# Gate-row riders moved to one per chunk, their total into the value stage, and a shorter rotation

## Chip, cores, metric

The kernel runs on one core of one Trainium2 chip. The metric is device time in microseconds (us) for one execution; lower is better.

## The reference

Two transformer-like blocks run on x of 256 tokens by 2048 features, in float32. The first block has two layers. Each modulates its normalised input and weighs its output with a gate that comes from a condition vector c:

```python
def first_block(x, c, ...):
    cond = jax.nn.silu(c)
    for i in range(DEPTH):                      # 2 layers: pool, then sparse attention
        mod = cond @ mod_w[i] + mod_b[i]
        shift, scale, gate = jnp.split(mod, 3, axis=-1)
        h = rms_norm(x, norm_g[i]) * (1.0 + scale[:, None, :]) + shift[:, None, :]
        ...
        x = x + gate[:, None, :] * out
    return rms_norm(x, final_g)

def rope_partial(x, positions, rot_dim):
    ...
    x1, x2, rest = xf[..., :half], xf[..., half:rot_dim], xf[..., rot_dim:]
    out = jnp.concatenate([x1 * cos - x2 * sin, x2 * cos + x1 * sin, rest], axis=-1)
```

The attention layer projects h to q, k, v, a gate (through silu) and indexer queries, keys and weights, rotates q, k and the indexer's parts, picks 64 keys per query and attends. The second block is an mLSTM branch and an attention branch side by side (q and k there are rotated over the whole head dimension of 128), and a feed-forward part with 8192 hidden features.

`mod_w[1]` has 2048 rows by 3 x 2048 columns. Its last third, times cond, is the gate row of the attention layer: the row that this change is about. It is needed first after attention, in the output projection.

## The kernel before

**Chunks and blocks.** All large products are float32 products made of three reduced-precision ones (high x high, low x high, high x low: L1890, L1891, L1892). A weight matrix comes in blocks of 2048 rows by 512 columns, a block in 8 chunks of 256 rows (512 KB). For each chunk SyncE issues the load into one of 8 slots of `raw` (L350), ScalarE writes the high part `w_hi` (L514), VectorE the low part `w_lo` (L1040), both with four slots, and TensorE multiplies. Queues are in order. ScalarE and VectorE work three chunks ahead of the block that TensorE is in (AHEAD = 3): a block's helper `blk` handles chunks 3 to 7 of its block and 0 to 2 of the next. In the code `o` counts 3 to 10; `hooks[o]` is other work put behind the parts of chunk o.

**Stages around the change.** idx_q (2 blocks), idx_kw (a narrow block of 80 columns), qk (8 blocks), gate (4), v (4), attention with 16 heads, attn_out. After each qk block ScalarE brings the result to `stage`, VectorE rotates it (`rotate`), and in the next block TensorE transposes it after chunk 3 and VectorE copies it out after its own chunk 5 (L1122).

**Riders.** The products of cond with `mod_w` that make shift and gate rows mostly don't run on TensorE. VectorE does them piece by piece between its low parts: a rider (L1282) takes a piece of 128 x 1024 (512 KB) from `ride_raw`, scales it by a value per partition and adds it to an accumulator, for this row `wide`. The row of unit 5 (the attention layer's gate row) has 32 riders, in the gate stage (RIDERS = {"gate": 5}). At the end `total_rows` adds up the 128 partitions with four products against ones (L2014, eight recorded matmuls), ScalarE copies the result to `wide` (L781) and stores it in four pieces to `gate_row`, from where it is later spread to all partitions.

**SyncE's queue in the gate stage.** `ride_raw` has four slots. The queue is in this order: the 8 weight loads of gate block 0, then rider loads 0 to 7, then for blocks 1 to 3 in turn weight load, rider load, weight load, rider load, and then the value stage's loads:

```python
            def ride(u, b, j):

                sp.wait_ge(mod_used, b * CPB + (RIDE[u] + j - 3))
                sp.dma_start(ride_raw[:, j % 4:j % 4 + 1, :], piece(u, b, j)).then_inc(ride_landed[j % 4], 16)
...
                    with sp.Fori(1, n) as b:
                        for j in range(CPB):
                            load(src, b, j, b + B0, cols=cols)
                            if u:
                                ride(u, b, j)
```

`mod_used` counts the riders done, so rider load c (c = 8b + j) waits until riders 0 to c-4 are done. A weight load waits for the low part that last used its slot, eight chunks back.

**VectorE in the gate stage.** `phase("gate")` first runs riders 0, 1 and 2 in a row, then the low part of chunk 3 and rider 3, the low part of chunk 4 and rider 4, and so on. In the last gate block riders stop at chunk 7, so that rider 31 is done ahead of the value stage's first chunks.

Of the kernel before, what the change touches and what calls it, by code (L numbers as in the profile page):

```python
# [9 lines left out]
ALU = mybir.AluOpType  # L10
# [4 lines left out]
NT = S // P  # L15
D = 2048
KC = D // P
NBLK = 512
KPC = 2
CPB = KC // KPC  # L20
RAW = 8
SPL = 4
AHEAD = 3
# [11 lines left out]
DSA_HEADS, MOBA_HEADS, M_HEADS, IDX_HEADS = 16, 8, 4, 16  # L35
# [79 lines left out]
JOBS, SPLITS = {}, {}  # L115
# [62 lines left out]
def build(nc, x, c, positions, norm_g, mod_w, mod_b, pool_w_in, pool_w_grp, pool_scale, pool_w_out, attn_w_in,  # L178
# [3 lines left out]
    with ExitStack() as ctx:  # L182
# [15 lines left out]
        tmp = sb("tmp", [P, 4, S])  # L198
        wide = sb("wide", [P, D])
# [24 lines left out]
        ps = ctx.enter_context(nc.psum_tensor("ps", [P, 8, 512], F32))  # L224
# [50 lines left out]
        tp_ready, tp_evac, xh_ready, x_ready = sem("tp_ready"), sem("tp_evac"), sem("xh_ready"), sem("x_ready")  # L275
# [8 lines left out]
        mod_taken, rows_ready, sum_rows = sem("mod_taken"), sem("rows_ready"), sem("sum_rows")  # L284
# [220 lines left out]
        def _(act):  # L505
            step = Chain(act, act_step)
# [48 lines left out]
            def blk(B, hooks=None, last=False, cols=NBLK, at=AHEAD):  # L555

                if hooks and AHEAD - 1 in hooks:
                    hooks[AHEAD - 1]()
                for o in range(at, CPB if last else CPB + AHEAD):
                    hi(B, o, cols if o < CPB else NBLK)  # L560
                    if hooks and o in hooks:
                        hooks[o]()
# [214 lines left out]
                to_qk(b, b + B0, b + A0)  # L777
            phase("gate", lambda b, B, A: evac(T2[:, :, bass.ds(b * NBLK, NBLK)], A, B * CPB + CPB, ACT.Silu))
            load_table(4, ACT.Exp)
            act.wait_ge(sum_rows, 2)  # L780
            nc.scalar.copy(wide[:, 0:NBLK], ps[:, 4, :]).then_inc(row_ready, 1)  # L781
            act.wait_ge(row_ready, 1)
            for q in range(4):
                act.dma_start(gate_row[:, q * NBLK:(q + 1) * NBLK], wide[32 * q:32 * q + 1, 0:NBLK]).then_inc(row_stored, 16)

            def copy_probs(h, i):

# [15 lines left out]
            def exp_hooks(h0):  # L803
                return {9: lambda: exps(h0, 0), 10: lambda: exps(h0 + 1, 1)}
# [16 lines left out]

            B0, A0, n = PHASES["v"]
            for b in range(n):
                blk(B0 + b, exp_hooks(0) if b == n - 1 else None)
                plain_evac(T3)(b, B0 + b, A0 + b)
            attention(0, DSA_HEADS, "attn", True, PHASES["attn_out"][0])

# [204 lines left out]
        def _(dve):  # L1032
# [44 lines left out]
                dve.wait_ge(x_ready, s + 1)  # L1077
                dve.sem_inc(tp_evac, 1)

            def blk(B, hooks=None, last=False, cols=NBLK, ride=None, b=None, ride_to=CPB + AHEAD, at=AHEAD):  # L1080


                if hooks and AHEAD - 1 in hooks:
                    hooks[AHEAD - 1]()
                for o in range(at, CPB if last else CPB + AHEAD):
                    lo(B, o, cols if o < CPB else NBLK)
                    if ride and o < ride_to:
                        rider(ride, b, o)
                    if hooks and o in hooks:
                        hooks[o]()  # L1090

            def phase(name, each=None, out=None, low=None, per=0, first=None, ahead=AHEAD):


                B0, A0, n = PHASES[name]
                u = RIDERS.get(name)
                if u:
                    for o in range(AHEAD):
                        rider(u, 0, o)
                blk(B0, first, ride=u, b=0, at=ahead)  # L1100
                if each:
                    each(0, A0)
                if n > 1:
                    def hooks(b):
                        return {5: lambda: out(b - 1), 6: lambda: low(b - 1)} if out else None

                    with step.loop(1, n - 1 if u else n, per) as b:
                        blk(b + B0, hooks(b), ride=u, b=b)
                        if each:
                            each(b, b + A0)  # L1110
                    if u:
                        blk(n - 1 + B0, hooks(n - 1), ride=u, b=n - 1, ride_to=CPB)
                        if each:
                            each(n - 1, n - 1 + A0)

            def leave(n, dst, scale=None, shift=None, bank=None):

# [85 lines left out]
            def rotate(src, heads, half, at):  # L1203

                v = src.rearrange("p t (h d) -> p t h d", h=heads)
                n = NT * heads * half
                ta, tb = (tmp[:].rearrange("p f t -> p (f t)")[:, k * 512:k * 512 + n]
                          .rearrange("p (t h d) -> p t h d", t=NT, h=heads) for k in range(2))
                x1, x2 = v[:, :, :, 0:half], v[:, :, :, half:2 * half]
                cosb, sinb = (rot[:, k, :, at:at + half].unsqueeze(2).to_broadcast([P, NT, heads, half])  # L1210
                              for k in range(2))
                step(tt(ta, x1, cosb, ALU.mult))
                step(tt(tb, x2, sinb, ALU.mult))
                step(tt(ta, ta, tb, ALU.subtract))
                step(tt(tb, x1, sinb, ALU.mult))
                step(tt(x2, x2, cosb, ALU.mult))
                step(tt(x2, x2, tb, ALU.add))
                step(nc.vector.tensor_copy(x1, ta))  # L1218


            cos, sin = rot[:, 0], rot[:, 1]
# [51 lines left out]
            def rider(u, b, o):  # L1273

                if o == 0 and isinstance(b, int):
                    dve.wait_ge(bias_landed, 16 * CLEARED[u])
                c0 = b * CPB + o
                at = o % 2 * 1024
                lap = b * 2 + (RIDE[u] // 4 + o // 4 + 1)
                dve.wait_ge(ride_landed[o % 4], lap * 16)  # L1280
                acc = mod_acc[u][:, at:at + 1024]
                stt(acc, ride_raw[:, o % 4, :], csil[:, bass.ds(b * 4 + o // 2, 1)], acc, ALU.mult, ALU.add  # L1282
                    ).then_inc(mod_used, 1)
                dve.wait_ge(mod_used, c0 + (RIDE[u] + 1))
# [181 lines left out]
            blk(B0, {3: start_scores, 6: ki_out, 9: lambda: index_scores(0)})  # L1466
            query_key(0, A0)
            dve.wait_ge(res_stored, 16)
            with step.loop(1, n, 11) as b:
                blk(b + B0, {3: lambda: qi_out_now(b), 5: lambda: qk_out(b - 1), 9: lambda: index_scores(b)})  # L1470
                query_key(b, b + A0)

# [246 lines left out]
            def aqk_out(b):  # L1719
                leave(b + JOBS["a_qk"], feat(2)[:, bass.ds(b * 4, 4), :])  # L1720

            phase("a_qk", rotary_full, aqk_out, lambda b: None, per=7,
                  first={2: lambda: mlstm_stage(0), 5: lambda: mlstm_stage(1), 9: lambda: mlstm_low(0, 6),
                         10: lambda: mlstm_low(1, 4)}, ahead=AHEAD + 2)
            B0, _, _ = PHASES["a_v"]
# [151 lines left out]
        def _(pe):  # L1877
# [43 lines left out]
            def blk(B, A, X, free, hooks=None, ready=None, half=None, at=0):  # L1921


                if hooks and -1 in hooks:
                    hooks[-1]()
                if free:
                    pe.wait_ge(acc_free, A - 1)
                for j in range(at, CPB):
                    if half and j == 0:
                        pe.wait_ge(x_first, half)  # L1930
                    elif ready is not None and j % 2 == (1 if half and j < 2 else 0):
                        pe.wait_ge(x_ready, ready + j // 2 + 1)
                    chunk(B, j, X, KPC * j, A, j == 0, j == CPB - 1)
                    if hooks and j in hooks:
                        hooks[j]()

            def phase(name, X, job=None, first=None, ready=None, half=None, at=0):

                B0, A0, n = PHASES[name]
                blk(B0, A0, X, A0 >= 2, first, ready, half, at)  # L1940
                if n > 1:
                    if A0 < 2:
                        blk(1 + B0, 1 + A0, X, False, {3: lambda: job(0)} if job else None)
                    with pe.Fori(2 if A0 < 2 else 1, n) as b:
                        blk(b + B0, b + A0, X, True, {3: lambda: job(b - 1)} if job else None)
# [64 lines left out]
            def total_rows(u, bank):  # L2010

                pe.wait_ge(mod_used, RIDE[u] + 2 * KC)
                for q in range(4):
                    ins = mm(ps[32 * q:32 * q + 32, bank, :], ones[:, 0:32], mod_acc[u][:, q * NBLK:(q + 1) * NBLK],  # L2014
                             start=True, stop=True)
                ins.then_inc(sum_rows, 1)
# [138 lines left out]
            with pe.Fori(1, n) as b:  # L2155
                blk(b + B0, b + A0, XB, True, {3: lambda: qk_job(b - 1), 5: lambda: index_scores(b)})
            phase("gate", XB, first={3: lambda: qk_job(7)})
            pe.wait_ge(tp_evac, JOBS["qk"] + 8)
            pe.wait_ge(relu_ready, IDX_HEADS)
            total_rows(5, 4)  # L2160

            def logits(h0, i, q, k, rows_of=1):
                h = h0 + i
# [53 lines left out]
            def dsa_logits(i):  # L2217
                if i == 0:
                    pe.wait_ge(row_ready, 1)
                logits(0, i, lambda i, r: qk_t[:, i, :], lambda i, r: qk_t[:, DSA_HEADS + i, :])  # L2220

            B0, A0, n = PHASES["v"]
            for b in range(n):
                blk(B0 + b, A0 + b, XB, True, {4: lambda: dsa_logits(0), 5: lambda: dsa_logits(1)} if b == n - 1 else None)
            attention(0, DSA_HEADS, "attn", dsa_logits, lambda i, u: T3[:, u, i * HD:(i + 1) * HD], exp_ready, 0,
                      PHASES["v"][1] + 4, 0, ahead("attn_out", XA, SPLITS["attn"]))
            norm2_job = stage_job("norm2")
# [198 lines left out]
```

## Time and the profile before

| | |
|---|---|
| median of 3 runs | 2392.73 us (2392.38 to 2394.37) |
| the profiled execution's own time | 2391.25 us |
| its span, first to last instruction | 2389.3 us |
| TensorE busy | 2338.3 us, 98% |
| VectorE busy | 1524.9 us, 64% |
| ScalarE busy | 1115.9 us, 47% |
| mean DMA rate | 221 GB/s |
| granted TensorE clock, mean | 0.994 |

In the profile PE is TensorE's matmuls, PEld its weight loads, DVE VectorE, ACT ScalarE, POOL GpSimd, SP SyncE; L1040 is line 1040 of the kernel. All times count from the span's start. The gate stage runs from about 641 to 730 us.

### The profile page before, as it was taken

The numbers are of one execution on the slowest core, as the hardware profiler recorded it, in microseconds if no ns is written. First come the engines' busy times: TensorE is split into PE (matmuls) and PEld (weight loads), VectorE is DVE, ScalarE is ACT, GpSimd is POOL, SyncE is SP. The second block draws the span as 40 slices with busy tenths as digits, with TensorE's granted clock in tenths as the row PEclk, the third lists the DMA queues.
The fourth block names the chain that finished last, engine by engine and source line by source line (L and its number), as shares of the span: only waits on it lengthen the run. The fifth ranks groups of instructions, "written<-read, shape, count | busy, mean of one in ns | idle before, by whom it ended". The sixth has DMA issues, their size and how long they took to land.

```text
span 2389.3 us, 30006 instructions
## 1 busy us (share of the span) xinstructions
PE 2338.3 (98%) x11030; PEld 1900.7 (80%) x11030; DVE 1524.9 (64%) x1837; ACT 1115.9 (47%) x1346; POOL 15.2 (1%) x21
## 2 busy tenths in 40 slices
PE   5999999999999999999999999999999999999997
PEld 1877777888788888888888888887888888888886
DVE  2988887666697566865664444665655565565555
ACT  2454445444344555544545444454544444444444
POOL 0000000000000000000000000000000000000000
PEclk8999999999999999999999999999999999999999
DMA  9999996555697445756554766555666656656653
GB/s 393 398 371 382 372 401 235 179 176 184 204 390 244 148 177 186 229 160 185 153 173 148 239 194 191 190 186 168 190 189 187 192 185 194 193 183 193 190 186 105
DMA packets 245077, 528.18 MB, mean 221 GB/s; under 512 B 20956, under 2 KB 21220, under 8 KB 241000
## 3 DMA queue, kind: packets, MB, share of 16 engines
q1 hardware_dynamic: 241376, 510.40, 64.4%
q0 software_dynamic: 1936, 13.67, 1.5%
q10 hardware_dynamic: 1656, 2.65, 0.3%
q8 instruction: 70, 1.15, 0.2%
q14 instruction: 39, 0.32, 0.0%
HBM read 520.35 MB, written 6.30 MB: 220 GB/s over the span
## 4 chain that ended last, share of the span: by engine, by line
PE 94%; DVE 3%; DMA 1%; ACT 1%; issue 1%; ACTq 0%; DVEq 0%
PE ps L1890 29%; PE ps L1892 29%; PE ps L1891 29%; PE ps L1959 2%; DMA ifb<-in_f_bias 1%; PE ps L1989 1%; PE ps L2168 0%; DVE w_lo L1040 0%; PE ps L2209 0%; PE ps L2068 0%; PE ps L2145 0%; ACT tmp L797 0%; PE ps L2211 0%; PE ps L2210 0%; ACTq L653 0%
## 5 line engine op out<-in xcount | busy, mean ns | idle before, releaser
L1040 DVE TENSOR_TENSOR w_lo<-raw,w_hi 128x1024 fp32r<-128x1024 f32 x784 | 945.3, 1218 | 479.5 <-ACT w_hi L514 463.1
L514 ACT CAST w_hi<-raw 128x1024 fp32r<-128x1024 f32 x784 | 814.3, 1046 | 830.4 <-PE ps L1892 785.6
L1890 PE MATMUL ps<-w_hi,xa_hi 128*128 128x512 f32 x2176 | 855.9, 393 | 4.4 <-DVE w_lo L1040 2.2
L1892 PE MATMUL ps<-w_hi,xa_lo 128*128 128x512 f32 x2176 | 847.5, 389 | 0.0
L1891 PE MATMUL ps<-w_lo,xa_hi 128*128 128x512 f32 x2176 | 846.9, 389 | 0.0
L1890 PEld LDWEIGHTS ps<-w_hi,xa_hi 128*128 128x128 f32 x2176 | 408.5, 188 | 98.0 <-issue 11.0
L1892 PEld LDWEIGHTS ps<-w_hi,xa_lo 128*128 128x128 f32 x2176 | 408.4, 188 | 85.8
L1891 PEld LDWEIGHTS ps<-w_lo,xa_hi 128*128 128x128 f32 x2176 | 408.7, 188 | 82.7
L1890 PE MATMUL ps<-w_hi,xb_hi 128*128 128x512 f32 x928 | 365.4, 394 | 1.7 <-issue 1.3
L1892 PE MATMUL ps<-w_hi,xb_lo 128*128 128x512 f32 x928 | 361.6, 390 | 0.0
L1891 PE MATMUL ps<-w_lo,xb_hi 128*128 128x512 f32 x928 | 361.3, 389 | 0.0
L1890 PEld LDWEIGHTS ps<-w_hi,xb_hi 128*128 128x128 f32 x928 | 174.2, 188 | 45.0 <-issue 8.8
L1892 PEld LDWEIGHTS ps<-w_hi,xb_lo 128*128 128x128 f32 x928 | 174.2, 188 | 36.6
L1891 PEld LDWEIGHTS ps<-w_lo,xb_hi 128*128 128x128 f32 x928 | 174.3, 188 | 35.1
L526 ACT ACTIVATE stage<-ps 128x1024 f32<-128x1024 f32 (+1 forms) x60 | 61.6, 1026 | 84.0 <-PE ps L1892 84.0
L1282 DVE SCALAR_TENSOR_TENSOR T<-T,csil 128x1024 f32<-128x1024 f32 x64 | 81.9, 1280 | 8.3 <-DMA T<-in_mod_w 6.1
L1282 DVE SCALAR_TENSOR_TENSOR wide<-T,csil,wide 128x1024 f32<-128x1024 f32 x64 | 81.9, 1279 | 0.5 <-DVE stage L1218 0.4
L1122 DVE COPY tmp<-ps 128x1024 f32<-128x1024 f32 x20 | 24.5, 1225 | 78.6 <-PE ps L1959 78.6
L1989 PE MATMUL ps<-T,csil 128*32 128x256 f32 (+1 forms) x384 | 44.8, 542 | 22.2 <-DMA T<-in_mod_w 22.2
L553 ACT CAST xa_hi<-tmp 128x1024 fp32r<-128x1024 f32 (+1 forms) x25 | 26.3, 1054 | 80.0 <-DVE tmp L1122 75.6
L1959 PE MATMUL ps<-con,stage 128*128 128x128 f32 x416 | 54.0, 273 | 0.0
L1959 PEld LDWEIGHTS ps<-con,stage 128*128 128x128 f32 x416 | 48.3, 140 | 6.5
(259 smaller groups left out, 978.8 us busy)
## 6 DMA issues: line engine op xcount, KB each, us to landing
raw<-in_w_in SPq DMA_DIRECT2D x176, 512.0 KB, 4.1
T<-in_mod_w SPq DMA_DIRECT2D x160, 512.0 KB, 7.3
raw<-in_attn_w_in SPq DMA_DIRECT2D x144, 512.0 KB, 4.6
raw<-in_w_up SPq DMA_DIRECT2D x128, 512.0 KB, 4.1
raw<-in_w_down SPq DMA_DIRECT2D x128, 512.0 KB, 4.5
raw<-in_pool_w_in SPq DMA_DIRECT2D x64, 512.0 KB, 7.7
T<-in_mod_w SPq DMA_DIRECT2D x16, 1024.0 KB, 9.0
raw<-in_pool_w_out SPq DMA_DIRECT2D x32, 512.0 KB, 8.4
```

The source lines that it names most:

```text
L514: nc.scalar.copy(w_hi[:, o % SPL, :, 0:cols], raw[:, o % RAW, :, 0:cols]).then_inc(hi_ready, 1)
L526: nc.scalar.activation(dst, ps[:, bass.ds((A % 2) * 2, 2), :], func).then_inc(acc_free, 1)
L553: nc.scalar.copy(X[0][:, bass.ds(g * 4, 4), :], src).then_inc(xh_ready, 1)
L1040: tt(w_lo[:, o % SPL, :, part], raw[:, o % RAW, :, part], w_hi[:, o % SPL, :, part].bitcast(F32), ALU.subtract).then_inc(lo_ready, 1)
L1122: nc.vector.tensor_copy(dst, src).then_inc(tp_evac, 1)
L1282: stt(acc, ride_raw[:, o % 4, :], csil[:, bass.ds(b * 4 + o // 2, 1)], acc, ALU.mult, ALU.add).then_inc(mod_used, 1)
L1890: mm(dst, x_hi, h, start=first and k == 0, stop=False)
L1891: mm(dst, x_hi, l, start=False, stop=False)
L1892: ins = mm(dst, x_lo, h, start=False, stop=last and k == KPC - 1)
L1959: ins = nc.tensor.transpose(dst, part, ident)
L1989: ins = mm(ps[32 * q:32 * q + 32, bank, at:at + n], col, src[:, q * n:q * n + n], start=first, stop=k == KC - 1, skip_group_check=True)
```

## The change

Four edits:

1. VectorE's riders of the gate stage: no riders ahead of the first block; rider k runs behind the low part of chunk k+3 instead of chunk k. The last three therefore run behind the low parts of the value stage's first three chunks, and the special last block goes.
2. TensorE's total of the row moves from between the gate and value stages to behind chunk 3 of the first value block.
3. ScalarE's copy and its four stores of the row move from between the stages to behind its high part 8 (o = 8) in the first value block. The table load (`load_table(4, ACT.Exp)`) stays.
4. `rotate` keeps a third product in an area of its own, writes both results in place and needs no last copy: six operations for seven, and the loops' step counts `per` follow (11 to 10, 7 to 6). The area is in `wide` where a product has 512 columns, else in `tmp`.

SyncE's program is not changed.

```diff
@@ ScalarE
             load_table(4, ACT.Exp)
-            act.wait_ge(sum_rows, 2)
-            nc.scalar.copy(wide[:, 0:NBLK], ps[:, 4, :]).then_inc(row_ready, 1)
-            act.wait_ge(row_ready, 1)
-            for q in range(4):
-                act.dma_start(gate_row[:, q * NBLK:(q + 1) * NBLK], wide[32 * q:32 * q + 1, 0:NBLK]).then_inc(row_stored, 16)
+
+            def last_gate():
+                act.wait_ge(sum_rows, 2)
+                nc.scalar.copy(wide[:, 0:NBLK], ps[:, 4, :]).then_inc(row_ready, 1)
+                act.wait_ge(row_ready, 1)
+                for q in range(4):
+                    act.dma_start(gate_row[:, q * NBLK:(q + 1) * NBLK], wide[32 * q:32 * q + 1, 0:NBLK]).then_inc(row_stored, 16)
...
             for b in range(n):
-                blk(B0 + b, exp_hooks(0) if b == n - 1 else None)
+                blk(B0 + b, exp_hooks(0) if b == n - 1 else None if b else {8: last_gate})
@@ VectorE, blk
                 for o in range(at, CPB if last else CPB + AHEAD):
                     lo(B, o, cols if o < CPB else NBLK)
-                    if ride and o < ride_to:
-                        rider(ride, b, o)
+                    if ride:
+                        rider(ride, b, o - AHEAD)
                     if hooks and o in hooks:
                         hooks[o]()
@@ VectorE, phase
                 u = RIDERS.get(name)
-                if u:
-                    for o in range(AHEAD):
-                        rider(u, 0, o)
                 blk(B0, first, ride=u, b=0, at=ahead)
...
-                    with step.loop(1, n - 1 if u else n, per) as b:
+                    with step.loop(1, n, per) as b:
                         blk(b + B0, hooks(b), ride=u, b=b)
                         if each:
                             each(b, b + A0)
-                    if u:
-                        blk(n - 1 + B0, hooks(n - 1), ride=u, b=n - 1, ride_to=CPB)
-                        if each:
-                            each(n - 1, n - 1 + A0)
@@ VectorE, rotate
-                ta, tb = (tmp[:].rearrange("p f t -> p (f t)")[:, k * 512:k * 512 + n]
-                          .rearrange("p (t h d) -> p t h d", t=NT, h=heads) for k in range(2))
+                flat = tmp[:].rearrange("p f t -> p (f t)")
+                ta, tb, tc = (v.rearrange("p (t h d) -> p t h d", t=NT, h=heads) for v in (
+                    flat[:, 0:n], flat[:, 512:512 + n], wide[:, 1024:1024 + n] if n == 512 else flat[:, 256:256 + n]))
...
                 step(tt(ta, x1, cosb, ALU.mult))
+                step(tt(tc, x1, sinb, ALU.mult))
                 step(tt(tb, x2, sinb, ALU.mult))
-                step(tt(ta, ta, tb, ALU.subtract))
-                step(tt(tb, x1, sinb, ALU.mult))
                 step(tt(x2, x2, cosb, ALU.mult))
-                step(tt(x2, x2, tb, ALU.add))
-                step(nc.vector.tensor_copy(x1, ta))
+                step(tt(x1, ta, tb, ALU.subtract))
+                step(tt(x2, x2, tc, ALU.add))
@@ TensorE
             phase("gate", XB, first={3: lambda: qk_job(7)})
-            pe.wait_ge(tp_evac, JOBS["qk"] + 8)
-            pe.wait_ge(relu_ready, IDX_HEADS)
-            total_rows(5, 4)
+
+            def last_gate():
+                pe.wait_ge(tp_evac, JOBS["qk"] + 8)
+                pe.wait_ge(relu_ready, IDX_HEADS)
+                total_rows(5, 4)
...
-                blk(B0 + b, A0 + b, XB, True, {4: lambda: dsa_logits(0), 5: lambda: dsa_logits(1)} if b == n - 1 else None)
+                blk(B0 + b, A0 + b, XB, True, {4: lambda: dsa_logits(0), 5: lambda: dsa_logits(1)} if b == n - 1 else None if b else {3: last_gate})
```

## Rows read from the trace of the kernel before

**Rows 1.** The page: busy time, and the chain that ended last, by engine.

```profile
PE 2338.3 (98%) x11030; PEld 1900.7 (80%) x11030; DVE 1524.9 (64%) x1837; ACT 1115.9 (47%) x1346; POOL 15.2 (1%) x21
...
PE 94%; DVE 3%; DMA 1%; ACT 1%; issue 1%; ACTq 0%; DVEq 0%
```

**Rows 2.** TensorE's waits over the span: us in total, times, longest.

```profile
PE ps L1890 <- DVE w_lo L1040: 2.6, 4, 1.0
...
PE ps L1905 <- DVE w_lo L1040: 0.7, 1, 0.7
```

**Rows 3.** Timeline of TensorE, gate stage: start, us, what [idle before]; x8 merged.

```profile
649.88 0.50 PE L1890 MATMUL ps<-w_hi,xa_hi 128*128 128x512 f32 x1 [0.91 <-DVE w_lo L1040]
...
652.74 1.03 PE L1959 MATMUL ps<-con,stage 128*128 128x128 f32 x8
...
729.88 1.07 PE L2014 MATMUL ps<-wide,con 128*32 128x512 f32 x8
730.87 0.50 PE L1890 MATMUL ps<-w_hi,xa_hi 128*128 128x512 f32 x1
```

**Rows 4.** Timeline of VectorE at the head of the gate stage.

```profile
643.70 0.29 DVE L1217 TENSOR_TENSOR stage<-stage,tmp 128x128 f32<-128x128 f32 x1
...
644.64 3.92 DVE L1282 SCALAR_TENSOR_TENSOR wide<-T,csil,wide 128x1024 f32<-128x1024 f32 x3 [0.39 <-DVE stage L1218]
648.60 1.22 DVE L1040 TENSOR_TENSOR w_lo<-raw,w_hi 128x1024 fp32r<-128x1024 f32 x1
649.74 1.28 DVE L1282 SCALAR_TENSOR_TENSOR wide<-T,csil,wide 128x1024 f32<-128x1024 f32 x1
651.06 1.23 DVE L1040 TENSOR_TENSOR w_lo<-raw,w_hi 128x1024 fp32r<-128x1024 f32 x1
...
655.97 1.23 DVE L1122 COPY T<-ps 128x1024 f32<-128x1024 f32 x1
657.11 1.21 DVE L1040 TENSOR_TENSOR w_lo<-raw,w_hi 128x1024 fp32r<-128x1024 f32 x1
```

**Rows 5.** Timeline of SyncE's queue: weight load 8, rider load 8, weight load 9.

```profile
651.75 0.40 SPq L350 DMA_DIRECT2D raw<-in_attn_w_in  x1
653.68 0.34 SPq L382 DMA_DIRECT2D T<-in_mod_w  x1
654.28 0.38 SPq L350 DMA_DIRECT2D raw<-in_attn_w_in  x1
```

**Rows 6.** Landing of weight loads issued 651.75, 656.68, 660.29, and 560 to 600.

```profile
DMA to landing us min/median/max: 4.3/4.3/4.3
...
DMA to landing us min/median/max: 5.8/5.8/5.8
...
DMA to landing us min/median/max: 4.8/4.8/4.8
...
DMA to landing us min/median/max: 3.4/3.6/4.8
```

**Rows 7.** Timelines of ScalarE and VectorE, high to low part of one chunk.

```profile
724.54 1.05 ACT L514 CAST w_hi<-raw 128x1024 fp32r<-128x1024 f32 x1 [1.50 <-PE ps L1892]
...
725.63 1.23 DVE L1040 TENSOR_TENSOR w_lo<-raw,w_hi 128x1024 fp32r<-128x1024 f32 x1 [1.26 <-ACT w_hi L514]
```

**Rows 8.** Windows: stretch, busy by engine (instructions), granted clock, DMA share, GB/s.

```profile
20.00:30.00 10.00, 6.31 (x32) 0.56 (x24) 4.71 (x13) 1.48 (x2) 0.00 (x0) 0.72 1.00 392
...
652.00:730.00 78.00, 78.00 (x352) 64.41 (x355) 71.67 (x60) 33.63 (x32) 0.00 (x0) 1.00 1.03 387
```

**Rows 9.** Timeline of VectorE at the end of a rotation of 512 columns.

```profile
1175.44 0.43 DVE L1218 COPY stage<-tmp 128x512 f32<-128x512 f32 x1
1176.20 3.49 DVE L1040 TENSOR_TENSOR w_lo<-raw,w_hi 128x1024 fp32r<-128x1024 f32 x3 [0.33 <-DVE stage L1218]
```

**Rows 10.** Timeline of VectorE in value block 0, around a top-8 round.

```profile
735.60 2.36 DVE L1040 TENSOR_TENSOR w_lo<-raw,w_hi 128x1024 fp32r<-128x1024 f32 x2 [6.03 <-ACT w_hi L514]
...
739.82 2.36 DVE L1040 TENSOR_TENSOR w_lo<-raw,w_hi 128x1024 fp32r<-128x1024 f32 x2
```

More of the change, by code:

```diff
@@ L1078, in low_job, with blk @@
                 dve.sem_inc(tp_evac, 1)
-            def blk(B, hooks=None, last=False, cols=NBLK, ride=None, b=None, ride_to=CPB + AHEAD, at=AHEAD):
+            def blk(B, hooks=None, last=False, cols=NBLK, ride=None, b=None, at=AHEAD):
                 if hooks and AHEAD - 1 in hooks:
@@ L1468, in _ @@
             dve.wait_ge(res_stored, 16)
-            with step.loop(1, n, 11) as b:
+            with step.loop(1, n, 10) as b:
                 blk(b + B0, {3: lambda: qi_out_now(b), 5: lambda: qk_out(b - 1), 9: lambda: index_scores(b)})
@@ L1720, in aqk_out @@
                 leave(b + JOBS["a_qk"], feat(2)[:, bass.ds(b * 4, 4), :])
-            phase("a_qk", rotary_full, aqk_out, lambda b: None, per=7,
+            phase("a_qk", rotary_full, aqk_out, lambda b: None, per=6,
                   first={2: lambda: mlstm_stage(0), 5: lambda: mlstm_stage(1), 9: lambda: mlstm_low(0, 6),
```

## The prediction

> **What bounds the kernel now.** I read the page first, then TensorE's waits, then the timelines around the only stage that the first part of the edit touches. On the page TensorE is busy 98% of the span and carries 94% of the chain that ended last [rows 1]. So whatever keeps TensorE supplied costs nothing, and whatever starves it is paid in full. TensorE's waits say how little there is to win by an easier VectorE: over the whole run the product L1890 waits 2.6 us for low parts in four places, and the narrow product L1905 waits 0.7 us once [rows 2].
>
> One of those four waits is at the head of the gate stage (gate chunk 3, 649.88, idle 0.91) [rows 3]. VectorE's timeline shows why: the last rotation of the query and key stage ends, three riders run in a burst for 3.92 us, and only then comes the low part of chunk 3 [rows 4]. I call gate chunks 0 to 31 and the value stage's first one 32. TensorE takes chunks 3 to 31 and eight transposes (1.03) from 649.88 to 729.88: (80.00 - 1.03) / 29 = 2.72 us a chunk. The four-product total (eight recorded matmuls) takes 729.88 to 730.87, 0.99, and then chunk 32 starts [rows 3]. VectorE starts a low part every 2.46 us (648.60 to 651.06), so it can catch up [rows 4].
>
> SyncE's queue is the third view. It holds, in order, weight load c, rider load c, weight load c+1. Rider load c waits until riders 0 to c-4 are done (four slots). In the trace rider 4 ends at 651.06 + 2.42 = 653.48; rider load 8 is issued at 653.68 and weight load 9 at 654.28 [rows 4, 5]. So a weight load is tied to a rider, though it has nothing to do with it.
>
> **The change, part by part.**
>
> *Burst removed.* TensorE's 0.91 us at chunk 3 goes: without 3.92 us of riders the low part of chunk 3 is long ready.
>
> *Riders three chunks later.* Rider k ran behind the low part of chunk k; now it runs behind that of chunk k+3. Their number stays 32. Follow it into the queue: weight load c+1 stands behind rider load c, which needs rider c-4, which now follows low part c-1. So weight load c+1 can't be issued before low part c-1 and its rider are done, and low part c+1 needs that load: a closed loop over **two** chunks. Before, rider c-4 followed low part c-4, a loop over five chunks, 13.6 us of TensorE time. Behind SyncE's waiting instruction stand all later weight loads; ScalarE's high part waits for them, then VectorE, then TensorE.
>
> The loop's time, step by step. Low part and rider: 648.60 to 649.74 + 1.28 = 651.02, so 2.42 [rows 4]. Rider's end to weight load issued: 651.02 to 651.75 and 653.48 to 654.28, mean 0.76 [rows 4, 5]. High part 1.05 and handover 0.04 (724.54 to 725.63) [rows 7]. With L from issue to landing: 4.27 + L. L isn't fixed. Weight loads of 512 KB near the head of the stage show 4.3, then up to 5.8 as pairs follow each other every 2.5 us, then 4.8 after a longer gap [rows 5, 6]. In the loop a pair comes every 4.4 us on average, near the first and last of these, and I take 4.5. The loop is then 8.77 us for two chunks where TensorE wants 5.44. The bounds: 3.4, the quickest load of the query and key stage, which has no rider load ahead of it, and 5.8 [rows 6].
>
> The Trainium skill, "DMA: Bandwidth & Descriptors" (Anatomy of one DMA), splits a transfer into about 2.0 us that don't depend on size and bytes at 436 GB/s: an estimate from that page is 3.2 us for 512 KB. The 3.4 us row agrees roughly. With the rider load's 1.2 us ahead, issued 0.6 us earlier, it would be 3.8, the loop 8.1, and the whole kernel about 2422 us. The same page's rule to issue early and wait late is what this edit gives up.
>
> *Where the loop starts.* The last multiply of the rotation ends at 643.99, and 0.39 later (the old gap from copy to burst) low part 3 starts at 644.38. Rider 2 ends 2 x 2.46 + 2.42 later, 651.72. Then VectorE has to copy out the last query/key job, whose transposes follow chunk 3 and end at 653.77 - 0.91 = 652.86; the copy starts at about 652.95, and low part 6 1.14 later (655.97 to 657.11) at 654.09 [rows 3, 4]. Rider 3 ends at 656.51, load 8 is issued at 657.24, lands at 661.74, low part 8 starts at 662.83 and ends at 664.05. TensorE, undisturbed, wants chunk 8 at 648.97 + 5 x 2.72 + 1.03 = 663.6. The eight buffered chunks are used up just there: no cover is left.
>
> *The sum.* Chunk 32 is twelve loops after chunk 8 (load 32 is the last behind a rider load). Its low part starts at 662.83 + 12 x 8.77 = 768.07, and TensorE starts it 1.22 + 0.06 later, 769.35. Before, it did so at 730.87 with the total ahead of it. The 0.99 us of the total come later now, so the comparison is with 729.88: **+39.5 us**, the 0.91 already in it.
>
> *Total, copy and row stores moved into value block 0.* The same four products, one copy and four stores of the row. The total no longer waits for the last rider: VectorE has passed low part 34 and rider 31 before TensorE reaches the hook after chunk 35. ScalarE's copy stands after its high part 8, which needed TensorE past the total. What queues behind it is one later high part; the first that wait for the row's stores (VectorE ahead of attention, POOL behind it) do so three blocks on. Cover in that block is thin because VectorE has no lead after the starvation, yet it needs 739.82 - 735.60 = 4.22 us for two chunks with a top-8 round, against 5.44, so it gains [rows 10]. At nothing; if the cover fails, about 1 us.
>
> *Rotations in six operations.* The copy L1218 goes in 15 rotations; the two results now go in place because a third product is kept. Of the fifteen, most end in front of a VectorE with lead. Where TensorE waited, the rotation counts: in the head-dimension-128 rotations of the second block, copy started 1175.44, the next low part 1176.20; without it that start is 0.33 after 1175.40, 0.47 us earlier [rows 9]. In the indexer's narrow block I credit 0.3 of the 0.7 us wait [rows 2]. Together -0.8. The wide third product needs `wide` free: its next filling comes after the attention of the second block.
>
> Sum against the profiled execution (2391.25, span 2389.3): 2391.25 + 39.5 - 0.8 = 2429.95. The median of runs is 1.5 above that execution: **2431 us**, about 1.6% slower.
>
> **Rivals.**
> - *The loop doesn't bind*, and only the small gains stay: 2392.73 - 0.91 - 0.8 = 2391.0, no slower than before. It decides where 4.27 + L is under 5.44, so L under 1.17 us. No row is under 3.4. It would need my reading of the queue to be wrong. For it speaks that the stage runs its 29 chunks after the first wait at an even 2.72 us [rows 3]; but there the loop has five chunks.
> - *The two interleaved loops meet at the DMA queues*, odd and even chunks, and every load takes 5.8: thirteen loads (load 8 and twelve loops) x 1.3 = +17, 2448. For it: 5.8 has been seen, under twice that traffic. Against: the stage's DMA engines are fully busy at 387 GB/s now [rows 8], and the loop would ask for 1 MB in 4.4 us, 240 GB/s.
> - *TensorE's clock falls in the new gaps.* When TensorE waited for transfers at 20 to 30 us, busy 6.31 of 10, the granted clock was 0.72 of full, a mix of the 1.2 and 2.4 GHz levels [rows 8]; the loop leaves TensorE 62% busy. At 0.72 a chunk is 3.8 us, still inside the loop's 4.4 a chunk: hidden. At 1.2 GHz throughout, 24 chunks take 131 us instead of 105: +25, 2457. It decides from a mean clock under 0.62. The Trainium skill, "TensorE: Matmul & The Clock Gate" (HAM oscillation), says that a loop waiting for a DMA in each step can be throttled anew in each step. By that rule alone this rival's upper end is 2457; the row at 20 us agrees that the clock falls, not that it stays down.
> - *A smaller loss*, 2395 to 2417, if L is under 3.4 or some loads get out early.
>
> **How the numbers follow.** The loop with L between 3.5 and 5.6: 0.76. Meeting loads 0.08, clock 0.06, smaller loss 0.05, no effect 0.05. Each 0.1 us of L is 1.3 us of time: L = 3.5 gives 2418, 5.6 gives 2445.6; I give 2418 to 2446. A difference under 0.2% (4.8 us) can't be told from none here. Slower 0.94 (the loop, its variants and the smaller loss, less a little), same 0.05, faster 0.01: all the waits that this edit could remove are under 0.2%.
>
> **What would show it.** In the profile after: TensorE's idle time before L1890 in the gate stage near 40 us, released by VectorE's low part; ScalarE's high parts waiting for `raw`; SyncE's rider loads waiting for the rider at nearly each step; low parts in pairs 8.8 us apart; GB/s near 240 there; the value stage back at 2.72 us a chunk. It is wrong if weight loads are issued without waiting for riders, if L is well off 4.5, or if the clock in the stage falls under 0.62. The last rotation copy gone, TensorE's wait near 1176 us should halve.

## The result, and the profile after

The changed kernel takes 2432.16 us (median of 6 runs, 2429.91 to 2434.37) against 2392.56 for the kernel before in the same runs: a ratio of 1.0165, with a 95% interval of 1.0155 to 1.0175. It is 39.6 us slower; the forecast was 2431, 1.6% slower. In the experiments, one of the ten executions of e2 took 4787.67 us, for a reason that no trace shows, and is left out of its ratio.

The page of the changed kernel, in the lines that answer to [rows 1]: the span, part 1, part 2's slices (about 61 us each), and the chain that ended last.

```profile
span 2429.7 us, 29993 instructions
...
PE 2355.6 (97%) x11030; PEld 1908.1 (79%) x11030; DVE 1520.5 (63%) x1822; ACT 1115.2 (46%) x1346; POOL 15.2 (1%) x21
...
PE   6999999999978999999999999999999999999997
...
PEclk8999999999989999999999999999999999999999
...
PE 89%; DMA 4%; DVE 3%; ACT 2%; issue 1%; ACTq 0%; SPq 0%; DVEq 0%
```

TensorE's slices in the kernel before, for comparison:

```profile
PE   5999999999999999999999999999999999999997
```

New is one place in which TensorE is short of work: slices 12 and 13 (668 to 790 us), which hold most of the gate stage and the head of the value stage. The clock is lower in slice 12. A transfer now makes 4% of the chain that ended last, where it was 1%, and ScalarE 2%.

Who waited between 640 and 800 us in the changed kernel (us in total, times, longest); line 1885 is the product that was 1890, line 1042 the low part:

```profile
ACT w_hi L514 <- DMA raw<-in_attn_w_in: 82.3, 25, 8.5
DVE w_lo L1042 <- ACT w_hi L514: 53.8, 25, 4.5
PE ps L1885 <- DVE w_lo L1042: 26.2, 13, 3.7
```

And SyncE's queue in the same stretch; line 382 is the rider load, 1277 the rider:

```profile
SPq L382 <- DVE wide L1277: 96.8, 28, 11.7
```

The same wait in the kernel before, between the same times, was half as long over as many rider loads, and TensorE did not feel it:

```profile
SPq L382 <- DVE wide L1282: 47.6, 28, 10.9
```

Read together they are the forecast loop: SyncE waits for a rider, ScalarE for the weight load behind it, VectorE for ScalarE, TensorE for VectorE, and the next rider stands behind that low part. One turn of it in SyncE's timeline (rider load 9, weight load 10) and in VectorE's:

```profile
665.99 0.33 SPq L382 DMA_DIRECT2D T<-in_mod_w  x1
666.57 0.38 SPq L350 DMA_DIRECT2D raw<-in_attn_w_in  x1
```

```profile
663.41 1.23 DVE L1042 TENSOR_TENSOR w_lo<-raw,w_hi 128x1024 fp32r<-128x1024 f32 x1 [3.81 <-ACT w_hi L514]
664.55 1.27 DVE L1277 SCALAR_TENSOR_TENSOR wide<-T,csil,wide 128x1024 f32<-128x1024 f32 x1
665.97 1.23 DVE L1042 TENSOR_TENSOR w_lo<-raw,w_hi 128x1024 fp32r<-128x1024 f32 x1
667.11 1.28 DVE L1277 SCALAR_TENSOR_TENSOR wide<-T,csil,wide 128x1024 f32<-128x1024 f32 x1
671.86 1.22 DVE L1042 TENSOR_TENSOR w_lo<-raw,w_hi 128x1024 fp32r<-128x1024 f32 x1 [3.47 <-ACT w_hi L514]
...
769.38 1.23 DVE L1042 TENSOR_TENSOR w_lo<-raw,w_hi 128x1024 fp32r<-128x1024 f32 x1 [2.85 <-ACT w_hi L514]
```

Low part 8 starts at 663.41, its rider ends at 665.82, weight load 10 is issued at 666.57, low part 10 starts at 671.86. At the head of the stage before, a low part came every 2.46 us [rows 4]; now they come in pairs, and ahead of each pair VectorE idles 2.9 to 4.5 us for ScalarE. The last row is chunk 32: (769.38 - 663.41) / 12 = 8.83 us a loop.

### The profile page after: what moved, and what is told of

Same layout as the page of the kernel before. It is cut to its first block, busy times and chain, and to the rows that moved or that the text cites. A ratio compares the mean times of both kernels' runs of the same rounds, so it can differ in the third digit from the quotient of the medians.

```text
span 2429.7 us, 29993 instructions
## 1 busy us (share of the span) xinstructions
PE 2355.6 (97%) x11030; PEld 1908.1 (79%) x11030; DVE 1520.5 (63%) x1822; ACT 1115.2 (46%) x1346; POOL 15.2 (1%) x21
## 3 DMA queue, kind: packets, MB, share of 16 engines
q8 instruction: 70, 1.15, 0.2%
## 4 chain that ended last, share of the span: by engine, by line
PE 89%; DMA 4%; DVE 3%; ACT 2%; issue 1%; ACTq 0%; SPq 0%; DVEq 0%
PE ps L1885 28%; PE ps L1887 28%; PE ps L1886 28%; PE ps L1954 2%; DMA raw<-in_attn_w_in 2%; DMA ifb<-in_f_bias 1%; PE ps L1984 1%; ACT w_hi L514 1%; DVE wide L1277 1%; DVE w_lo L1042 1%; PE ps L2165 0%; PE ps L2206 0%; PE ps L2063 0%; ACT tmp L799 0%; PE ps L2140 0%
## 5 line engine op out<-in xcount | busy, mean ns | idle before, releaser
L1885 PE MATMUL ps<-w_hi,xa_hi 128*128 128x512 f32 x2176 | 862.1, 396 | 29.3 <-DVE w_lo L1042 27.0
L1885 PEld LDWEIGHTS ps<-w_hi,xa_hi 128*128 128x128 f32 x2176 | 410.9, 189 | 129.1 <-DVE w_lo L1042 26.6
L1885 PE MATMUL ps<-w_hi,xb_hi 128*128 128x512 f32 x928 | 365.4, 394 | 1.6 <-issue 1.3
L1885 PEld LDWEIGHTS ps<-w_hi,xb_hi 128*128 128x128 f32 x928 | 174.2, 188 | 45.6 <-issue 9.2
```

Source lines behind the costliest of these rows:

```text
L1885: mm(dst, x_hi, h, start=first and k == 0, stop=False)
```

## The experiments

"Before" in each is the kernel before, timed beside it on the same chip. All edits but those of e4 and e9 are made to the changed kernel.

**e1: the queue's order alone.** SyncE issues rider load c-3 behind weight load c.

```diff
-                    for j in range(CPB):
+                    for j in range(CPB - 3):
                         ride(u, 0, j)
...
                             load(src, b, j, b + B0, cols=cols)
                             if u:
-                                ride(u, b, j)
+                                ride(u, b if j >= 3 else b - 1, (j - 3) % CPB)
```

The last three rider loads stand behind the value stage's first three weight loads.

> The changed kernel with SyncE's queue alone reordered: rider load c-3 stands behind weight load c, instead of rider load c; VectorE, ScalarE and TensorE as in the changed kernel. My theory (a closed loop weight load - high part - low part - rider - rider load - next weight load over two chunks): the loop is over five chunks again, 13.6 us against about 9, and doesn't bind; only the small gains stay: 2392.6 - 0.9 - 0.8 = 2391, within 2389 to 2394. TensorE's wait in the gate stage gone. Rival (the later riders, the moved total or the thinner lead of VectorE cost by themselves): the time stays at 2415 to 2432.

Measured: 2392.07 against 2393.26, ratio 0.9996 (0.9987 to 1.0005). The whole loss is gone with the riders as late as in the changed kernel and the total in the value block. TensorE's window in e1 (columns as in [rows 8]) shows no idle time:

```profile
662.00:760.00 98.00, 98.00 (x437) 80.21 (x436) 84.11 (x114) 45.59 (x45) 0.00 (x0) 1.00 0.94 342
```

The same window of the changed kernel:

```profile
662.00:760.00 98.00, 75.15 (x275) 56.49 (x273) 53.25 (x44) 27.31 (x27) 0.00 (x0) 0.90 0.67 235
```

**e2 and e3: how late the riders are.** Rider k behind the low part of chunk k+2 (e2) or k+1 (e3), with one or two riders ahead of the stage; SyncE as in the changed kernel.

```diff
                 if u:
+                    for o in range(AHEAD - LAG):     # LAG = 2 in e2, 1 in e3
+                        rider(u, 0, o)
...
-                    if ride:
-                        rider(ride, b, o - AHEAD)
+                    if ride and o < ride_to:         # in the last block CPB + LAG
+                        rider(ride, b, o - LAG)
```

> The changed kernel with rider k behind the low part of chunk k+2 (one rider ahead of the stage). SyncE as before. My theory: the loop is over three chunks, 8.17 us of TensorE, and takes 4.27 + L; with more traffic than in the changed kernel L is 4.8 to 5.8, so 9.1 to 10.1; over 24 chunks +7 to +15, less 2.7 for one chunk more of cover and 1.7 for the small gains: 2395 to 2405, best guess 2399. Rival (the cost grows evenly with how late the riders come): two thirds of 40 us, about 2419.

> The changed kernel with rider k behind the low part of chunk k+1 (two riders ahead of the stage). My theory: a loop over four chunks, 10.9 us of TensorE, against at most 10.1: it doesn't bind, 2391 to 2393. Rival (cost grows evenly with the lag): about 2405.

Measured: e2 2397.57 against 2393.26, ratio 1.0021 (1.0012 to 1.0031); e3 2390.59 against 2393.26, ratio 0.9991 (0.9982 to 1.0000). Two steps of lag cost 7 us over e3, the third step 35 us more. That is no even cost of lateness; it fits a loop that starts to bind at three chunks. VectorE's timeline in e2, low parts 8 and 32:

```profile
660.12 1.22 DVE L1043 TENSOR_TENSOR w_lo<-raw,w_hi 128x1024 fp32r<-128x1024 f32 x1 [1.06 <-ACT w_hi L515]
...
733.09 1.22 DVE L1043 TENSOR_TENSOR w_lo<-raw,w_hi 128x1024 fp32r<-128x1024 f32 x1 [0.69 <-ACT w_hi L515]
```

(733.09 - 660.12) / 8 = 9.12 us for three chunks, against 8.17 that TensorE needs: the low end of the expected 9.1 to 10.1.

**e4: the rotation alone**, in the kernel before.

> The kernel before with the rotation in six operations alone. My reckoning: -0.8 us (0.47 where a rotation of 512 columns keeps TensorE waiting near 1176 us, 0.3 in the narrow block near 448), plus 0.3 at the head of the gate stage, where the rotation stands ahead of the burst: 2391.4 against 2392.5. Rival: no difference, since TensorE's waits move elsewhere.

Measured: 2391.58 against 2393.26, ratio 0.9994 (0.9985 to 1.0003). It goes the way expected, but by itself is not clear of no difference.

**e5: is the lower clock part of the price?**

```diff
-            phase("gate", XB, first={3: lambda: qk_job(7)})
+            def awake_free(n):
+                for _ in range(n):
+                    mm(ps[:, 7, 0:P], ident, ident, start=True, stop=True)
+
+            B0, A0, n = PHASES["gate"]
+            blk(B0, A0, XB, True, {3: lambda: qk_job(7)})
+            with pe.Fori(1, n) as b:
+                blk(b + B0, b + A0, XB, True, {j: (lambda: awake_free(5)) for j in range(CPB)})
```

> The changed kernel with five extra products of 128 x 128 by 128 columns behind each chunk of gate blocks 1 to 3, into a free accumulator bank (extra work, nothing of the computation changed): about 1.1 us a chunk, so that TensorE needs 3.8 us a chunk in a loop that gives it 4.4. My theory: the lower granted clock of the changed kernel's gate stage (0.83 to 0.96) is hidden inside the loop, so that the time stays within 2 us of the changed kernel's 2432, while the clock of the stage rises towards 1.0 or stays. Rival (the 17 us by which TensorE's busy time grew are part of the price): 2415 to 2422 if the clock stays up.

Measured: 2431.46 against 2393.01, ratio 1.0163 (1.0149 to 1.0177), the time of the changed kernel. Its window:

```profile
662.00:760.00 98.00, 91.31 (x490) 76.34 (x489) 54.48 (x46) 27.20 (x27) 0.00 (x0) 1.00 0.71 233
```

The granted clock is back at 1.00 (from 0.90), TensorE is busy 91 us instead of 75, and the time doesn't move (the interval is 3.4 us to either side). So neither the lower clock nor TensorE's work has a part in the price that these runs could tell from nothing, and the 17 us of the rival are excluded; the slower products sat inside the loop.

**e6: one place back in the queue.** As e1, but rider load c-1 behind weight load c: the loop is over three chunks with the riders as late as in the changed kernel.

> The changed kernel with rider load c-1 behind weight load c in SyncE's queue, the riders themselves as late as in the changed kernel. My theory: a loop over three chunks, as with rider k behind low part k+2, so the same time as that one, 2395 to 2405. Rival (the riders' lateness costs, whatever the queue's order): 2425 to 2432.

Measured: 2397.43 against 2393.01, ratio 1.0018 (1.0008 to 1.0027). This is e2's time within 0.2 us, reached from SyncE's side. What the two have in common, and e1, e3 and the changed kernel do not have, is a loop over three chunks.

**e7: riders as before**, total and rotation as changed (e2's edit with a lag of 0).

> The changed kernel with riders as in the kernel before (three in a burst, rider k behind low part k), keeping the moved total, copy and stores, and the shorter rotation. My theory: the move of the total costs nothing and brings nothing; the rotation brings 0.8 and 0.3 of the head's 0.9 wait: 2391.4. Rival: the total inside the value block makes a wait of its own, 2393 to 2396.

Measured: 2391.48 against 2393.01, ratio 0.9995 (0.9986 to 1.0004). The moved total makes no wait that can be measured.

**e8: the old rotation**, riders and total as changed.

> The changed kernel with the old rotation in seven operations: riders and total as changed. My theory: the whole slowdown is here, 2432 to 2434. Rival: the rotation has a hidden cost of its own (its third product in another area), and the time falls below 2430.

Measured: 2432.48 against 2393.01, ratio 1.0165 (1.0150 to 1.0181). So the slowdown is not in the rotation. By e7 it is not in the moved total either, which leaves the riders' edit.

**e9: the slowdown without touching VectorE.** In the kernel before, SyncE's rider loads move three places forward.

```diff
-                    for j in range(CPB):
-                        ride(u, 0, j)
+                    for j in range(CPB + 3):
+                        ride(u, j // CPB, j % CPB)
...
                             load(src, b, j, b + B0, cols=cols)
                             if u:
-                                ride(u, b, j)
+                                ride(u, b if j < 5 else b + 1, (j + 3) % CPB)
```

In the last block the rider loads past 31 are left away, since there are none.

> The kernel before with SyncE's queue alone changed: in the gate stage rider load c+3 stands behind weight load c, so that weight load c+1 stands behind the wait for rider c-1, which follows low part c-1. VectorE, ScalarE and TensorE as before: riders with their burst, total between the stages, old rotation. My theory: the same two-chunk loop of 8.8 us without any rider moved. It starts about 3 us later than in the changed kernel (the burst) and holds weight loads 8 to 29 only: chunk 28 starts at about 754.8 instead of 719.0, so +36: 2429, within 2422 to 2436. Rival (the riders' lateness or VectorE's order costs): no change from 2392.6.

Measured: 2431.43 against 2393.49, ratio 1.0156 (1.0139 to 1.0172). No rider, product or copy is moved, and the loss is there. Low parts 8 and 28 in VectorE's timeline:

```profile
668.60 1.22 DVE L1045 TENSOR_TENSOR w_lo<-raw,w_hi 128x1024 fp32r<-128x1024 f32 x1 [3.47 <-ACT w_hi L519]
...
757.94 1.23 DVE L1045 TENSOR_TENSOR w_lo<-raw,w_hi 128x1024 fp32r<-128x1024 f32 x1 [3.36 <-ACT w_hi L519]
```

(757.94 - 668.60) / 10 = 8.93 us, the same loop. TensorE could start chunk 28 at 757.94 + 1.28 = 759.2, 4.4 us later than I had reckoned (754.8). Of this 3.15 us is this execution's own: its rotation starts at 645.22, not 642.07, and it is as late at 562 us, far ahead of the gate stage. The other 1.3 us is the loop, ten turns of 8.93 for 8.77, less a start that without the 3.15 is 0.4 earlier than reckoned. The median time is 2.4 us above the best guess and inside the range.

**e10: one term of the loop made smaller.**

```diff
-                stt(acc, ride_raw[:, o % 4, :], csil[:, bass.ds(b * 4 + o // 2, 1)], acc, ALU.mult, ALU.add
-                    ).then_inc(mod_used, 1)
+                n = 512 if u == 5 else 1024
+                stt(acc[:, 0:n], ride_raw[:, o % 4, 0:n], csil[:, bass.ds(b * 4 + o // 2, 1)], acc[:, 0:n], ALU.mult, ALU.add
+                    ).then_inc(mod_used, 1)
```

> The changed kernel with each gate-stage rider working on 512 of its 1024 columns (half of the gate row's products are left out; all loads as they are). A rider then takes about 0.65 us instead of 1.28. My theory: the rider is a term of the loop, which is 0.6 us shorter: twelve loops and the start give -8, 2424 (2421 to 2427). Rival (the stage is bound by the DMA queues or by TensorE's clock): no change, 2430 to 2433. Were VectorE's busy time the bound, 24 chunks x 0.63 = -15, 2417.

Measured: 2423.87 against 2393.49, ratio 1.0126 (1.0109 to 1.0143): 8.3 us less than the changed kernel. VectorE's timeline, rider 4, low part 8 and low part 32:

```profile
658.41 0.75 DVE L1278 SCALAR_TENSOR_TENSOR wide<-T,csil,wide 128x512 f32<-128x512 f32 x1
663.25 1.23 DVE L1042 TENSOR_TENSOR w_lo<-raw,w_hi 128x1024 fp32r<-128x1024 f32 x1 [4.08 <-ACT w_hi L514]
...
763.44 1.22 DVE L1042 TENSOR_TENSOR w_lo<-raw,w_hi 128x1024 fp32r<-128x1024 f32 x1 [1.53 <-ACT w_hi L514]
```

The rider takes 0.75 instead of 1.28, 0.53 less, and the loop (763.44 - 663.25) / 12 = 8.35 instead of 8.83, 0.48 less. Twelve loops give 5.8. From low part 3 to low part 8 it is 17.41 us (645.84 to 663.25) instead of 18.19 (645.22 to 663.41), 0.8 more: 6.6 in all. This can't be set against the 8.3 directly, for the traced execution is the slowest of the four (2426.87; the others took 2423.57 to 2424.12), 4.8 us below the traced one of the changed kernel. Why its gain and the median's differ from 6.6 is open. VectorE idles 4.08 us for a load in front of low part 8, so it is not short of time: what shrank is the way round, once for two chunks and not once for each.

## Why the prediction was right, point by point

**TensorE is the bound, what starves it is paid in full.** Right. Over the whole run L1885's waits for low parts grew from 2.6 us in 4 places [rows 2] to 27.4 in 16.

**The queue ties weight load c+1 to rider c-4, a loop over two chunks.** Right, and shown from both sides: e1 and e6 lengthen it in the queue, e2 and e3 at VectorE, and e9 closes it in the kernel before. The rule to issue early and wait late, from the Trainium skill, "DMA: Bandwidth & Descriptors" (Rules for kernel authors), is borne out by e1: the same transfers, with the weight loads issued ahead of the rider loads' waits, cost nothing.

**The loop's time, 4.27 + L = 8.77.** Measured 8.83. L was the chosen term, 4.5. The 25 weight loads in flight between 662 and 765 us of the changed kernel (KB each, median us to landing):

```profile
raw<-in_attn_w_in SPq DMA_DIRECT2D x25, 512.0 KB, 4.4
```

Single ones took 4.0 to 5.2 while the loop ran, within the bounds of 3.4 and 5.8 [rows 6]. That 4.5 was near is partly luck: it was a choice between those bounds, and each 0.1 us of it is 1.3 us of time. The estimate of 3.8 worked out from the Trainium skill's "DMA: Bandwidth & Descriptors" (Anatomy of one DMA) was 0.6 us too short; the measurement decides. That section gives its figures for transfers issued from GpSimd, and these loads are issued from SyncE, which the prediction did not say.

**Where the loop starts, and the sum.** I put the start of low part 8 at 662.83 and of low part 32 at 768.07. In the changed kernel's own profile all of the stage is 0.92 us later (the rotation starts at 642.99, not 642.07; in e2's profile it starts at 642.05, so this is that execution's own); without these the two are 662.49 and 768.46. TensorE starts chunk 32 at 770.75: 770.75 + 0.99 - 730.87 - 0.92 = +39.95 against the forecast +39.5. Two small misses partly cancel here: the loop started 0.34 us earlier than reckoned, and its twelve turns took 0.73 us longer. The step from the traced execution to the median was 0.5 us where I had added 1.5, and this hid the 0.92.

**Total, copy and row stores at nothing.** Right: e7. ScalarE's copy and its stores in value block 0 of the changed kernel:

```profile
786.91 0.58 ACT L783 COPY wide<-ps 128x512 f32<-128x512 f32 x1
787.51 1.15 ACTq L786 DMA_DIRECT2D gate_row<-wide  x4
788.76 1.05 ACT L514 CAST w_hi<-raw 128x1024 fp32r<-128x1024 f32 x1 [1.28 <-PE ps L1887]
```

The high part behind them starts 1.28 us after the copy, released by TensorE, and the issuing (1.15) fits into that time. The last of TensorE's 13 waits for a low part is the one at 770.75: up to 800 us the value stage has none, as forecast.

**The rotation, -0.8.** Between 1164 and 1350 us TensorE's wait for a low part is 0.6 us where it was 1.0, in the narrow block 0.4 where it was 0.7 [rows 2]: together 0.7. The first was to halve and fell by 0.4. Each is seen in the profile; the time of e4 (-1.7, the interval reaches past zero) neither shows nor denies a value so small.

**The rivals.** The loop that doesn't bind would have needed L under 1.17: it was 4.4. Meeting loads at 5.8 didn't come. The clock is where one of the marks I had named was off. I wrote that TensorE's idle time in the stage would be near 40 us; it was 26. Windows of the changed kernel, columns as in [rows 8]:

```profile
662.00:680.00 18.00, 14.99 (x58) 11.58 (x57) 9.68 (x8) 6.39 (x6) 0.00 (x0) 0.91 0.67 239
680.00:700.00 20.00, 14.24 (x50) 10.90 (x49) 9.68 (x8) 5.06 (x5) 0.00 (x0) 0.83 0.65 230
```

The granted clock was at the lower of its two levels for part of the time, after gaps of up to 3.7 us: a mean of 0.83 in the second window. Near 675 us products start every 0.43 us, which is the 1.2 GHz level, and just before and after every 0.23, which is the 2.4 GHz one. TensorE's busy time over the kernel grew by 17.3 us with the same 11030 products, and this filled part of the gaps. The price was as forecast because the mean stayed above 0.62, the point where I had put the rival; e5 finds no part of the 39.6 us that was the clock's, within its 3.4 us. "TensorE: Matmul & The Clock Gate" of the Trainium skill (HAM oscillation) warns of such throttling in loops that wait for a DMA. The clock did fall here, not in each turn and not for good, and no cost of it could be measured.

## What to carry to other kernels

When two streams of loads share one in-order queue, each wait in it ties both. Count, in steps of the consumer, how far behind the newest finished work the queue's wait lets the next load be issued, and compare steps x time per step with the whole way round (wait, issue, landing, casts): here 5 and 4 steps were free, 3 cost 4 to 7 us, 2 cost 40. Whoever moves work later on one engine can keep the loop's length by moving its loads later in the queue by as much (e1). More slots for the riders' data, or a queue of their own for their loads, were not tried. Looking for cover on the engines alone misses the loop, for VectorE and ScalarE had time to spare (busy 63% and 46%).

None of the versions is clearly faster than the kernel before: e3 is lowest with 0.9991 (0.9982 to 1.0000). What the edit could win was 1.7 us of waits.

## What the runs showed of the hardware

- A lower granted clock (0.90 between 662 and 760 us) cost nothing measurable where a loop through the transfers set the pace: five small products a chunk brought it to 1.00, and the time was 2431.46 for 2432.16 (e5).
- ScalarE's wait for weight loads says little by itself. Between 650 and 735 us it was 33.6 us in the kernel before, with TensorE waiting 0.9; in e1 ScalarE waits for no weight load between 655 and 765 us, and the time is the same within 0.1%. In the changed kernel it was 82.3 us between 640 and 800 us, and TensorE waited 26.2. My reading, not tested by itself, is that the difference lies in whether the engines behind ScalarE had used up their lead.
